# Both feed-forward output projections of a two-block transformer, by column halves with seven-product pairs

## The chip, the cores and the metric

The kernel runs on one core of a Trainium2 chip. The metric is the device time of one execution in microseconds. TensorE (PE) does the matrix products, VectorE (DVE) and ScalarE (ACT) the element-wise work, GpSimd (POOL) issues the DMAs that add while they write, and SyncE (SP) issues most loads.

## What is computed

The reference is two transformer blocks at 256 tokens and width 2048, all in float32: mixers, cross-attention and a feed-forward network in each, with a scaled residual and a layer norm behind each. The parts that matter here are the output projections of the feed-forward networks (inner width 5632):

```python
# first block
h = x @ ffn_in
gate, up = split(h, 2)
gate = causal_conv3(gate) + conv_b
ff = (silu(gate) * up) @ ffn_out            # [256, 5632] @ [5632, 2048]
x = layer_norm(2 ** 0.25 * x + ff, g, b)
# second block
y = (silu(x @ w1) * (x @ w3)) @ w2          # [256, 5632] @ [5632, 2048]
x = layer_norm(2 ** 0.25 * x + y, g, b)
```

## The kernel before

**Units.** Every weight matrix is read in units of 512 rows by 512 columns (1 MiB). SP loads a unit into one of four slots of `wraw`; ACT writes its rounded high part into `whi` (`hi`, line 748); DVE subtracts and writes the low part into `wlo` (`lo`, line 2005); PE multiplies. A product in full precision takes three passes: high by high, high by low, low by high. A whole unit of the output projection is 4 row chunks by 2 token tiles (of 128 tokens) by 3 passes, 24 matmuls of 128x512 (line 1288, in `products`). Slot reuse ties the engines together: the high part of unit n waits until PE has finished unit n - 4 (`unit_done`), the load of unit n until the low part of n - 4 is written (`lo_done`). All engines run their instructions in order, and each engine's order is written out by hand.

**Input projections.** The hidden layer is made in eleven blocks of 512 features. From the second block on, seven products of half-size blocks stand for eight (`seven_products`, `part_products`, line 1409): some units hold weights that are sums of two weight blocks, made by POOL with an adding DMA (lines 1988 and 1990) or by DVE (`part_a <- part_a, wraw`), and some products take mixes of the activations (`mix_x`, `mix_h`, `mix_l`). Each block is written to `hidden_dram` by `send_hidden` (line 986).

**Output projection, before.** `ffn(...)` ends with eleven pieces of four units. Piece n is the hidden block n, read back into one of two `h_stage` tiles (`load_stage`, line 990, on ACT's queue), copied to the high part `f_h` (line 2546) and subtracted to the low part `f_l2` by `split_piece` on DVE. A piece is multiplied with four units, one for each 512 output columns (`cb` 0 to 3), into eight banks of PSUM, two a column block. All eight banks fill over the 44 units, so the results of all columns come at the end. DVE then adds them to the residual (`joined`, line 2181, in the first block; line 3003 in the second), takes the statistics (lines 2177, 3004) and normalises (lines 2203 and 2208; 3011 and 3012). In the first block four joins stand one behind each of the last four units, and between them three low parts of the next stage. In the second block the last four units are multiplied for the first token tile first and then for the second, so that DVE can finish the first tile meanwhile.

`dve.link` is an instruction with a wait for its own completion. `to_act` (DVE) is this:

```python
def to_act(ins):
    ins.then_inc(shifted, 1)
    lo_to(ahead[0])
    dve.wait_ge(mapped, w.at("mapped"))
```

Of the kernel before, what the change touches and what calls it, by code (L numbers as in the profile page):

```python
# [21 lines left out]
P = 128  # L22
T = 256
# [25 lines left out]
          ("mix_out", 16), ("xq", 4), ("xv", 4), ("xo", 4), ("ffn_in", 8 + 11 * (FB - 1)), ("ffn_out", 4 * FB),  # L49
          ("gates2", 1), ("mlstm", 16), ("mlstm1", 16), ("dilated", 24), ("out2", 16), ("x2", 48), ("xo2", 16),  # L50
          ("ffn2_in", 8 + 11 * (FB - 1)), ("ffn2_out", 4 * FB)]
# [14 lines left out]
def part(layer, i, j):  # L66

    return BASE[IN[layer]] + 8 + 11 * (i - 1) + j

# [137 lines left out]
def two_blocks(nc, a, tables, out):  # L207
    tab_at, _ = shape_tables()
    ctx = ExitStack()
    with ctx:  # L210
# [5 lines left out]
        def sem(name):  # L216
# [29 lines left out]
                   "x3": (X0, Y1), "x4": (Y1 + 12 * KB, Y1 + 20 * KB), "x5": (Y1 + 12 * KB, Y1 + 20 * KB),  # L246
                   "y": (X0, Y1)}
# [89 lines left out]
        up_t = place("up_t", Y1 + 20 * KB, [P, NT, UNIT])  # L337
        h_stage = [place(f"h_stage{n}", X0 + (8 + 4 * n) * KB, [P, CB, T]) for n in range(2)]
# [103 lines left out]
        first_tap = sem("first_tap")  # L442
        taps_made = sem("taps_made")
# [115 lines left out]
        def _(sp):  # L559
# [84 lines left out]
            def ffn(layer, gate, up, up_c, down):  # L644
# [27 lines left out]
                for cb in range(NB):  # L672
                    if cb == 0:
                        sp.wait_ge(fourth_sum_made, nth(layer, FB - 1))
                    else:
                        sp.wait_ge(lo_done, part(layer, FB - 1, (0, 6, 9, 11)[cb]))
                    load(rows(down, 0, cb * UNIT))
                with sp.Fori(1, FB) as i, w.loop(i, 1, FB - 1, {"unit": 4}):
                    for cb in range(NB):
                        load(down[bass.ds(i * UNIT, UNIT), cb * UNIT:(cb + 1) * UNIT].rearrange("(k p) n -> p k n", p=P))  # L680
# [55 lines left out]
        def _(act):  # L736
# [251 lines left out]
            def load_stage(layer, n):  # L988
                act.wait_ge(hidden_out, 16 * (FB * layer + n + 1))
                act.dma_start(h_stage[n % 2][:, :, :], hidden_dram.ap()[n]).then_inc(stage_in[n % 2], 16)  # L990
# [39 lines left out]
            def ffn(layer, following):  # L1030
# [22 lines left out]
                for i in range(1, FB):  # L1053
                    last = i == FB - 1

                    def next_high(j):
                        hi(1) if last else hi_part(layer, i + 1, j)
# [26 lines left out]
                    next_high(1)  # L1084
                    next_high(2)
# [7 lines left out]
                for n in range(2, FB):  # L1093
                    act.wait_ge(hidden_ready, FB * layer + n - 1)
                    load_stage(layer, n)
                    hi(1)
                    if n == 2 and not layer:
                        copy_up_and_tap(FB - 1, (4, 5), (6, 7))
                    hi(1)
                    if n == 2:  # L1100
                        if layer:
                            copy_hidden(FB - 1, (6, 7))
                        else:
                            map_taps(FB - 1)
                    elif n == 3 and not layer:
                        send_product(FB - 1)
                    hi(2)
                    if n == 4:
                        gains_for(following)
                        if following == "x3":  # L1110
                            small(b_hot[:, :], tab("hot")[0:REL, :])
                            small(b_rel[:, :], a["rel_bias_2"])
                hi(4)
# [141 lines left out]
        def _(pe):  # L1255
# [465 lines left out]
            def ffn(layer, first_of):  # L1721
# [9 lines left out]
                def piece(fresh, last, parity):  # L1731
                    pe.wait_ge(hidden_ready, w.at("hidden"))
                    for cb in range(NB):
                        if fresh:
                            if cb == 0:
                                pe.wait_ge(gates_kept, nth(layer, FB - 1))
                                pe.wait_ge(gates_read, nth(layer, FB - 1))
                            elif cb == 1:
                                pe.wait_ge(ups_read, 2 * nth(layer, FB - 1))
                                if not layer:  # L1740
                                    turn_block(layer, FB - 1, (4, 5), (6, 7))
                            elif cb == 2:
                                if layer:
                                    turn_block(layer, FB - 1, (), (6, 7))
                                else:
                                    pe.wait_ge(turned_copied, 2 * (FB - 1))
                            elif layer:
                                pe.wait_ge(turned_copied, 2 * nth(layer, FB - 1))
                            else:
                                pe.wait_ge(taps_made, CB * FB)  # L1750
                        products(T_BLOCK, 1, f_h[parity], f_l2[parity], cb * 1024, fresh=fresh, last=last)

                piece(True, False, 0)
                with pe.Fori(0, FB // 2 - 1) as i, w.loop(i, 0, FB // 2 - 1, {"unit": 8, "hidden": 2}):
                    piece(False, False, 1)
                    piece(False, False, 0)
                piece(False, False, 1)
                if not layer:
                    piece(False, True, 0)
                    return  # L1760
# [1297 lines left out]
```

## Time and profile before

| | |
|---|---|
| median of 3 runs | 3223.89 us (3223.07 to 3224.68) |
| the profiled execution's own time | 3227.49 us |
| its span in the trace | 3225.5 us |
| granted TensorE clock | 0.997 of full speed |
| busy: PE, DVE, ACT, POOL | 99%, 70%, 45%, 2% of the span |
| mean DMA rate | 220 GB/s |

The span runs from the first to the last instruction that the profile shows. Matmul ends are modelled and overlap, so that the distance from one matmul's start to the next says what a stream costs, not the length of one.

### The profile page before, as it was taken

To read this page: it belongs to the slowest core of one execution; us is meant where nothing else is said; L and a number is where in the kernel's file an instruction comes from. 1 tells how busy PE (TensorE), PEld (TensorE's weight loads), DVE (VectorE), ACT (ScalarE), POOL (GpSimd) and SP (SyncE) were. 2 spreads that over 40 slices of the span, in tenths; PEclk is the share of its full clock that TensorE was granted. 3 is DMA by queue.
4 is the path that set the end of the run, shared out by engine and by line. 5 is a ranking of instruction groups with operands and counts; after the bars stand their busy time and mean duration, and the time that the engine had idled before them with its cause. 6 is when DMAs were issued, how large, how long until landed. Compare 5 with 4: busy or idle time off the path is not lost.

```text
span 3225.5 us, 37942 instructions
## 1 busy us (share of the span) xinstructions
PE 3184.1 (99%) x16157; PEld 2696.9 (84%) x16157; DVE 2244.0 (70%) x1857; ACT 1442.4 (45%) x1032; POOL 52.2 (2%) x44
## 2 busy tenths in 40 slices
PE   9999999999999999999999999999999999999998
PEld 8888888888888888888888888888888888888886
DVE  7565566667678888885565786775555888888456
ACT  4333555433335666653333443343333555555332
POOL 0000000000000000000000000000000000000000
PEclk9999999999999999999999999999999999999999
DMA  8644556678558888877646455655546698888763
GB/s 315 214 166 159 196 183 228 216 261 294 174 195 250 268 262 265 255 249 246 221 156 223 151 180 199 219 208 170 170 170 209 192 277 259 262 260 282 250 216 114
DMA packets 312494, 708.34 MB, mean 220 GB/s; under 512 B 12392, under 2 KB 18324, under 8 KB 301332
## 3 DMA queue, kind: packets, MB, share of 16 engines
q1 hardware_dynamic: 270000, 587.50, 52.5%
q0 software_dynamic: 21120, 41.95, 7.4%
q10 hardware_dynamic: 21220, 76.66, 6.3%
q8 instruction: 118, 1.93, 0.2%
q14 instruction: 36, 0.29, 0.0%
HBM read 675.65 MB, written 30.41 MB: 219 GB/s over the span
## 4 chain that ended last, share of the span: by engine, by line
PE 92%; DVE 5%; DMA 1%; ACT 1%; issue 0%; ACTq 0%; DVEq 0%
PE ps L1409 44%; PE ps L1288 43%; PE ps L1283 4%; PE ps L1413 2%; DVE wlo L2005 1%; DMA wraw<-in_xattn_v 0%; DMA part_a<-in_ffn_in 0%; DVE tok L2241 0%; DVE tok L2246 0%; ACT whi L748 0%; DVE wlo L2509 0%; DVE tok L3012 0%; DVE act_hl L2069 0%; DVE tok L3011 0%; DMA s_b<-in_sg_ln_b 0%
## 5 line engine op out<-in xcount | busy, mean ns | idle before, releaser
L2005 DVE TENSOR_TENSOR wlo<-wraw,whi 128x2048 fp32r<-128x2048 f32 (+1 forms) x389 | 879.8, 2275 | 465.5 <-ACT whi L748 462.0
L748 ACT ACTIVATE whi<-wraw 128x2048 fp32r<-128x2048 f32 (+1 forms) x389 | 735.5, 1901 | 921.6 <-PE ps L1288 609.6
L1288 PE MATMUL ps<-whi,act_hl 128*128 128x512 f32 x2128 | 661.7, 392 | 1.4 <-DVE wlo L2005 1.1
L1409 PE MATMUL ps<-whi,act_hl 128*128 128x512 f32 x1808 | 557.2, 389 | 1.8 <-DVE f_b L2069 1.8
L1288 PEld LDWEIGHTS ps<-whi,act_hl 128*128 128x128 f32 x2128 | 396.1, 188 | 84.3 <-issue 1.9
L1288 PE MATMUL ps<-wlo,act_hl 128*128 128x512 f32 x1064 | 414.4, 389 | 0.0
L1409 PEld LDWEIGHTS ps<-whi,act_hl 128*128 128x128 f32 x1808 | 338.9, 188 | 73.2 <-DVE f_b L2069 2.2
L1409 PE MATMUL ps<-wlo,act_hl 128*128 128x512 f32 x904 | 351.8, 389 | 0.0
L1409 PE MATMUL ps<-act_hl,whi 128*128 128x512 f32 (+2 forms) x1376 | 306.8, 360 | 0.6 <-DVE m_k L2116 0.6
L2509 DVE TENSOR_TENSOR wlo<-wraw,whi 128x2048 fp32r<-128x2048 f32 x120 | 274.5, 2288 | 33.6 <-ACT whi L983 32.3
L983 ACT ACTIVATE whi<-wraw 128x2048 fp32r<-128x2048 f32 x120 | 230.0, 1916 | 150.3 <-PE ps L1409 131.4
L1409 PEld LDWEIGHTS ps<-act_hl,whi 128*128 128x128 f32 (+1 forms) x1376 | 240.0, 191 | 36.0 <-DVE m_k L2116 0.7
L1288 PE MATMUL ps<-whi,f_h 128*128 128x512 f32 x672 | 261.7, 389 | 0.2 <-DVE gate_t L2069 0.2
L1288 PE MATMUL ps<-wlo,f_h 128*128 128x512 f32 x672 | 261.5, 389 | 0.0
L1288 PE MATMUL ps<-whi,f_l 128*128 128x512 f32 x672 | 261.4, 389 | 0.0
L1288 PEld LDWEIGHTS ps<-wlo,act_hl 128*128 128x128 f32 x1064 | 199.7, 188 | 42.0
L1288 PE MATMUL ps<-whi,alt_hl 128*128 128x512 f32 x736 | 227.6, 390 | 0.0
L2509 DVE TENSOR_TENSOR wlo<-part_a,whi 128x2048 fp32r<-128x2048 f32 x80 | 183.3, 2291 | 61.5 <-ACT whi L983 60.8
L983 ACT ACTIVATE whi<-part_a 128x2048 fp32r<-128x2048 f32 x80 | 153.1, 1914 | 114.4 <-PE ps L1409 69.6
L1409 PEld LDWEIGHTS ps<-wlo,act_hl 128*128 128x128 f32 x904 | 169.7, 188 | 35.2
L1409 PE MATMUL ps<-act_hl,wlo 128*128 128x256 f32 x1136 | 171.5, 283 | 0.0
L1409 PEld LDWEIGHTS ps<-act_hl,wlo 128*128 128x128 f32 x1136 | 157.3, 190 | 4.8
(361 smaller groups left out, 3831.1 us busy)
## 6 DMA issues: line engine op xcount, KB each, us to landing
wraw<-in_w_in SPq DMA_DIRECT2D x118, 1024.0 KB, 5.4
wraw<-in_w SPq DMA_DIRECT2D x112, 1024.0 KB, 5.3
wraw<-laid_narrow_units SPq DMA_DIRECT2D x68, 1024.0 KB, 4.9
wraw<-in_ffn_in SPq DMA_DIRECT2D x68, 1024.0 KB, 7.4
wraw<-in_ffn_out SPq DMA_DIRECT2D x44, 1024.0 KB, 5.1
wraw<-in_w_branch SPq DMA_DIRECT2D x16, 1024.0 KB, 5.1
wraw<-in_w_mix_out SPq DMA_DIRECT2D x16, 1024.0 KB, 7.1
wraw<-in_w_out SPq DMA_DIRECT2D x16, 1024.0 KB, 5.3
```

The source lines that it names most:

```text
L748: act.activation(whi[:, slot, k, c], wraw[:, slot, k, c], ACT.Copy).then_inc(hi_done, 1)
L983: act.activation(whi[:, (g - 1) % SLOTS], part_raw(layer, i, j), ACT.Copy).then_inc(hi_done, 1)
L1283: ins = pe.matmul(o, wk, x, start=first and n == 0, stop=stop and n == 2, skip_group_check=True)
L1288: ins = pe.matmul(o, x, wk, start=first and n == 0, stop=stop and n == 2, skip_group_check=True)
L1409: return pe.matmul(o, left, right, start=start, stop=stop, skip_group_check=True)
L1413: return pe.matmul(o, src, ident[0:k, 0:k], start=True, stop=True, is_transpose=True, skip_group_check=True)
L2005: dve.tensor_tensor(wlo[:, slot, k, c], wraw[:, slot, k, c], whi[:, slot, k, c].bitcast(F32), ALU.subtract).then_inc(lo_done, 1)
L2509: dve.tensor_tensor(wlo[:, slot], part_raw(layer, i, j), whi[:, slot].bitcast(F32), ALU.subtract).then_inc(lo_done, 1)
```

## The change

Each output projection is done in two column halves, x = 0 (columns 0 to 1023) and x = 1 (1024 to 2047), of 28 units each. In a half, seven of the eleven hidden blocks (0, 1, 4, 5, 6, 9, 10) are whole pieces with two units of 24 matmuls. The other four make two pairs, (2, 3) and (7, 8). A pair with its two column blocks is a product of 2 by 2 blocks (two token tiles, two hidden blocks, two column blocks), and is done in seven products of 12 matmuls instead of eight. Units 4, 6, 7, 9, 11, 13, 14 of a half belong to the first pair and 18, 20, 21, 22, 24, 25, 26 to the second. The four banks of the half gather the sums of products for the result; the other half's four banks are the spare ones and gather the products that enter several results. At the end of the half `combine` on DVE adds and subtracts the spare sums into `tok`, together with the residual; `join` adds the half's own banks.

The weights of a pair: SP loads two blocks into `sum_o` and `part_c`; POOL adds a block to each with an adding DMA; DVE adds a third and fourth to `sum_o` (`add_to_sum`). The high part of a piece moves from DVE to ACT (`piece_rounded`, `pair_rounded`), and the activation mixes of a pair are made on DVE (`pair_low`), rounded on ACT (`mixes_rounded`) and subtracted on DVE (`out_mixes_low`). The hidden blocks are read back once for each half, 22 a projection instead of 11.

The core of the diff:

```diff
-          ... ("ffn_out", 4 * FB),
+          ... ("ffn_out", 2 * 28),
+WHOLE_AT = ((1, 2), (3, 5), (8, 10), (12, 15), (16, 17), (19, 23), (27, 28))
+SEVEN_AT = ((4, 6, 7, 9, 11, 13, 14), (18, 20, 21, 22, 24, 25, 26))
+WHOLE_PIECES = (0, 1, 4, 5, 6, 9, 10)
+SEVEN_PIECES = ((2, 3), (7, 8))
# SP, for each half x
+    if x: sp.wait_ge(out_fourth_made, seven_nth(layer, 0, 1))
+    load_whole(0, 0); load_whole(0, 1); load_first(0); load_second(0); load_whole(1, 0)
+    ...
+    load_whole(3, 0)
+    sp.wait_ge(out_third_made, seven_nth(layer, x, 0))
+    load(rows(down, SEVEN_PIECES[0][1] * UNIT, c0))
+    load_second(1)
# ACT
 def load_stage(layer, n):
+    piece = n % FB
+    act.wait_ge(hidden_out, 16 * (FB * layer + piece + 1))
+    if n > 1:
+        x, used = divmod(n - 2, FB)
+        if used in WHOLE_PIECES:
+            act.wait_ge(hidden_ready, whole_nth(layer, x, WHOLE_PIECES.index(used)))
+        else:
+            g = used // 5
+            act.wait_ge(pair_ready, seven_nth(layer, x, g))
+            act.wait_ge(out_mixes_made, seven_nth(layer, x, g))
# ACT, for each half x
+    load_stage(layer, begun + 2); piece_rounded(layer, x, 1); hi(1)
+    load_stage(layer, begun + 3)
+    ...
+    pair_rounded(layer, x, 0); hi_sum(layer, x, 0, 2)
+    load_stage(layer, begun + 4); load_stage(layer, begun + 5); mixes_rounded(layer, x, 0)
+    hi_sum(layer, x, 0, 3); hi(1); piece_rounded(layer, x, 2)
+    ...
+    hi(1); hi_sum(layer, x, 1, 1); pair_rounded(layer, x, 1)
+    load_stage(layer, begun + 9); load_stage(layer, begun + 10); mixes_rounded(layer, x, 1)
+    hi(1); piece_rounded(layer, x, 5)
# PE, for each half x
+    piece(0, 0)
+    if x: pe.wait_ge(combined, 2 * layer + 1)
+    else: pe.wait_ge(ups_read, 2 * nth(layer, FB - 1)); turn_block(layer, FB - 1, (4, 5), (6, 7))
+    piece(0, 1); piece(1, 0)
+    if x: pe.wait_ge(columns_joined, 2 * layer + 1)
+    pe.wait_ge(pair_ready, seven_nth(layer, x, 0))
+    seventh(tokens_in_pair(0, 0), spare, 0)
+    piece(1, 1)
+    if x: pe.wait_ge(columns_joined, 2 * layer + 2)
+    pe.wait_ge(out_mixes_ready, seven_nth(layer, x, 0))
+    seventh(mix(0), spare + 3, 0); seventh(mix(2), spare + 1, 0)
+    ...
# DVE
+def pair_low(layer, x, g):
+    dve.wait_ge(pair_high, 2 * m)
+    (two tensor_tensor subtractions into pair_l, the second signals pair_ready)
+    (four linked tensor_tensor subtractions into out_x, the last signals out_mixes_made)
+def combine(layer, x):
+    (waits for unit 24; eight linked 128x512 operations)
# DVE, for each half x
+    piece_low(layer, x, 1); lo(1)
+    pair_low(layer, x, 0); lo_sum(layer, x, 0, 2); out_mixes_low(layer, x, 0)
+    ...
+    lo(3); lo_sum(layer, x, 1, 1); pair_low(layer, x, 1); out_mixes_low(layer, x, 1)
+    lo(1); piece_low(layer, x, 5)
+    ...
+    lo_sum(layer, x, 1, 5); lo(1); add_to_sum(layer, x, 1, 6, out_fourth_made); lo_sum(layer, x, 1, 7)
+    piece_low(layer, x, 6); lo(2); combine(layer, x)
+    if x == 0:
+        lo(1); piece_low(layer, 1, 0); lo(2)
+        for half in range(2):
+            join(layer, 0, half, columns_joined)
+            statistics(tok, half)
+            if half == 0: lo_sum(layer, 1, 0, 1)
# POOL, for each half and pair
+    pool.wait_ge(out_c_in, ...);  part_c += block  (out_second_in)
+    pool.wait_ge(lo_done, out_unit(layer, x, SEVEN_AT[g][0]));  sum_o[g] += block  (out_first_in)
# DVE, behind the first block's projection
-    for cb in range(NB):
-        joined(tok, cb, ...)
-        statistics(tok, cb)
-        if cb < NB - 1: lo_to(w.now("unit") + 1 + cb)
+    lo_to(BASE["gates2"] + 1)
+    for half in range(2):
+        join(0, 1, half, sums_read)
+        statistics(tok, 2 + half)
+        if half == 0: lo_to(BASE["gates2"] + 2)
     ahead[0] = BASE["gates2"] + 3
     norm("x3", tok, act_h, act_l, ...)
# DVE, behind the second block's projection
-        for cb in range(NB):
+        for cb in range(2, NB):
```

## Rows read from the trace of the kernel before

**Rows 1.** The page: span, busy time and instructions of two engines.

```profile
span 3225.5 us, 37942 instructions
PE 3184.1 (99%) x16157; PEld 2696.9 (84%) x16157; DVE 2244.0 (70%) x1857; ACT 1442.4 (45%) x1032; POOL 52.2 (2%) x44
```

**Rows 2.** The chain that ended last (start, length, what): both output projections and their ends.

```profile
1308.27 40.82 PE ps L1409 x180
...
1428.36 233.98 PE ps L1288 x1032
1662.34 0.02 issue
...
2984.17 206.76 PE ps L1288 x912
3190.94 10.89 PE ps L1409 x48
```

**Rows 3.** Windows: an input projection's blocks, then the output projection (second block).

```profile
core 0: us, PE busy (x) PEld busy (x) DVE busy (x) ACT busy (x) POOL busy (x), PEclk, DMA share, GB/s
2652.00:2902.00 250.00, 250.00 (x1129) 207.45 (x1128) 206.94 (x121) 144.98 (x102) 15.60 (x12) 1.00 0.89 265
2984.00:3190.00 206.00, 206.00 (x911) 170.56 (x910) 103.56 (x56) 73.19 (x40) 0.00 (x0) 1.00 0.63 216
```

**Rows 4.** DMA queues, 1093 to 1349 us (six blocks of the first input projection); issues, KB, us to landing.

```profile
q1 hardware_dynamic: 25357, 50.36, 55.9%
q0 software_dynamic: 6336, 12.58, 28.3%
q10 hardware_dynamic: 864, 3.15, 3.0%
...
part_c<-in_ffn_in POOLq DMA_DIRECT2D x6, 1024.0 KB, 13.8
```

**Rows 5.** Tile `h_stage`: its DMAs' time to landing over the whole run (22 DMAs).

```profile
DMA to landing us min/median/max: 5.0/5.3/10.9
```

**Rows 6.** Timeline of DVE: low parts, old split of a piece, add, join, statistics.

```profile
1386.94 2.29 DVE L2069 TENSOR_TENSOR part_a<-part_a,wraw 128x2048 f32<-128x2048 f32 x1
1413.54 0.69 DVE L2546 CAST f_h<-h_stage 128x1024 fp32r<-128x1024 f32 x1
1414.27 1.22 DVE L2069 TENSOR_TENSOR f_l<-h_stage,f_h 128x1024 fp32r<-128x1024 f32 x1
1415.53 4.49 DVE L2005 TENSOR_TENSOR wlo<-wraw,whi 128x2048 fp32r<-128x2048 f32 x2
...
1646.05 1.22 DVE L2181 SCALAR_TENSOR_TENSOR tok<-tok,ps 128x1024 f32<-128x1024 f32 x1 [1.14 <-PE ps L1288]
1647.30 1.43 DVE L2177 BATCH_NORM_STATS2 bst<-tok 128x6 f32<-128x512 f32 x2
```

**Rows 7.** Timeline of DVE at the end of the first block's projection.

```profile
1659.64 2.29 DVE L2005 TENSOR_TENSOR wlo<-wraw,whi 128x2048 fp32r<-128x2048 f32 x1
1662.37 1.22 DVE L2181 SCALAR_TENSOR_TENSOR tok<-tok,ps 128x1024 f32<-128x1024 f32 x1 [0.43 <-PE ps L1288]
...
1665.67 0.17 DVE L2196 TENSOR_SCALAR rstd<-mv 128x2 f32<-128x2 f32 x1
1666.11 0.17 DVE L2197 RECIPROCAL rstd<-rstd 128x2 f32<-128x2 f32 x1 [0.27 <-ACT rstd L776]
```

**Rows 8.** Timeline of ACT: the high part of a unit, and an operation of a piece's size.

```profile
1389.27 1.93 ACT L983 ACTIVATE whi<-part_a 128x2048 fp32r<-128x2048 f32 x1 [2.88 <-DVE part_a L2069]
1402.80 1.07 ACT L1024 ACTIVATE h_block<-h_block 128x1024 f32<-128x1024 f32 x1 [3.19 <-DVE h_block L2558]
```

**Rows 9.** Timeline of DVE at the kernel's end.

```profile
3201.93 0.69 DVE L3003 SCALAR_TENSOR_TENSOR tok<-tok,ps 128x512 f32<-128x512 f32 x1 [1.30 <-PE ps L1409]
3202.65 0.69 DVE L3004 BATCH_NORM_STATS2 bst<-tok 128x6 f32<-128x512 f32 x1
3203.38 0.26 DVE L3005 BATCH_NORM_AGGREGATE mv<-bst 128x2 f32<-128x24 f32 x1
...
3210.10 0.68 DVE L3003 SCALAR_TENSOR_TENSOR tok<-tok,ps 128x512 f32<-128x512 f32 x1
...
3215.90 0.26 DVE L3005 BATCH_NORM_AGGREGATE mv<-bst 128x2 f32<-128x24 f32 x1
```

More of the change, by code:

```diff
@@ L1092, in ffn @@
                     next_high(4)
-                for n in range(2, FB):
-                    act.wait_ge(hidden_ready, FB * layer + n - 1)
-                    load_stage(layer, n)
+                for x in range(2):
+                    begun, spare = FB * x, 4 * (1 - x)
+                    load_stage(layer, begun + 2)
+                    piece_rounded(layer, x, 1)
                     hi(1)
-                    if n == 2 and not layer:
+                    load_stage(layer, begun + 3)
+                    if x + layer == 0:
@@ L1098, in ffn @@
                         copy_up_and_tap(FB - 1, (4, 5), (6, 7))
-                    hi(1)
[L1100 to L1105, printed above, removed]
+                    elif x == 0:
+                        copy_hidden(FB - 1, (6, 7))
+                    pair_rounded(layer, x, 0)
+                    hi_sum(layer, x, 0, 2)
@@ L1729, in ffn @@
                     seven_products(layer, i)
[L1731 to L1751, printed above, removed]
@@ L1758, in ffn @@
                 if not layer:
-                    piece(False, True, 0)
                     return
-                pe.wait_ge(hidden_ready, w.at("hidden"))
+                pe.wait_ge(hidden_ready, whole_nth(1, 1, 6))
                 for h in range(NT):
-                    for cb in range(NB):
-                        unit = w.now("unit") - NB + cb + 1 if h else w.at("unit")
+                    for half in range(2):
+                        unit = w.now("unit") - 1 + half if h else w.at("unit")
@@ L2550, in taps, with join @@
+            def join(layer, x, half, signal):
+                cb = 2 * x + half
+                dve.wait_ge(unit_done, out_unit(layer, x, WHOLE_AT[6][half]))
+                tt(tok[:, cb], tok[:, cb], two(ps[:, cb * 1024:cb * 1024 + 1024]), ALU.add).then_inc(signal, 1)
             def taps(n, gate, dst):
@@ L2647, in ffn @@
                     next_low(4)
[L2648 to L2649 removed]
+                for x in range(2):
+                    piece_low(layer, x, 1)
                     lo(1)
[L2651 removed]
+                    if x + layer == 0:
                         taps(FB - 1, turned_gate((6, 7)), h_block)
[L2653 to L2657 removed]
@@ L2661, in _ @@
+                w.at("unit", out_unit(layer, 1, 28) - w.now("unit"))
             for q in range(NB):
```

407 lines of the change are left out of this document (356 added, 51 removed).

## Prediction

> **What bounds the kernel now.** I read the page first: PE is busy 99% of the span, DVE 70% [rows 1]. Then the chain that ended last, at the two places that the change touches. From 1428.36 the chain is PE alone for 1032 matmuls in 233.98 us, and from 2984.17 for 912 in 206.76: 0.2267 us a matmul, with no gap [rows 2]. (One matmul lasts 0.39 us in the lists, but they overlap; the pitch is the cost.) So a whole unit costs 24 x 0.2267 = 5.44 us of PE, a unit of a seven-product pair 2.72 us. The windows say how much room the others have: beside the output projection DVE is busy 103.56 of 206 us and DMA 0.63 of its time; beside the input projection, where seven products stand for eight already, DVE 206.94 of 250 and DMA 0.89, and PE still has no gap [rows 3]. The clock is full in both, so no clock effect is in the sum.
>
> **What is removed.** Before, 44 x 24 = 1056 matmuls a projection; after, per half 14 x 24 + 14 x 12 = 504, so 1008. 48 fewer, 10.9 us each, 21.8 us for both projections.
>
> **Is there still room?** Per half PE has 504 x 0.2267 = 114.3 us. DVE's prices: a low part follows the next by 2.20 us (two in 4.49), an add of the same size 2.2, a piece's low part 1.2, join 1.25, statistics 1.46 [rows 6]; a linked 128x512 operation 0.72 (3201.93 to 3202.65, [rows 9]). Per half: 28 low parts 61.6, four adds 8.8, two mix low parts 4.4, seven piece low parts 8.4, two pairs of 2 x 1.2 + 4 x 0.72 = 10.6, combine 8 x 0.72 = 5.8; 99.6 us, and 5.4 more for joins and statistics at x = 0. That is 92% of PE's time. DMA: in six input blocks 48 loads of SP take 55.9% of 256 us, 3.0 us each; 12 adding ones 28.3%, 6.0 us each; six of 0.5 MiB 3.0%, 1.3 us each [rows 4]. A half has 22, 4 and 11 of these: 65.6 + 24.1 + 14.1 = 103.8 of 114.3 us, 91%. The sums fit, barely, so what counts is the order.
>
> **Walk through a half.** Time 0 is the start of unit 1; ends at full pace: unit 8 at 35.4, 14 at 57.2, 18 at 76.2, 21 at 87.1, 24 at 98.0, 25 at 100.7, 26 at 103.4, 27 at 108.9, 28 at 114.3. A high part (1.9 us, [rows 8]) of n can start at the end of n - 4. I go by these and by the orders of the front.
>
> *Entry, x = 0.* The old split of piece 0 loses its 0.7 us copy on DVE; the stage of block 3 is requested when piece 1's low part is ready, about 6 us in, and its pair is wanted by unit 4 at 16.3 (later in the first block, by the 1.75 us of turns). With a landing of 5 to 8 us it fits. Its taps (3.2 us) fit too. Cost 0.
>
> *Second pair.* Low part 18 ends at 57.2 + 1.9 + 2.2 = 61.3; pair low parts and mixes to 66.5. Only then is block 9's stage requested. Landing L, rounding 1.05, low part 1.2: ready at 68.9 + L against unit 19 at 76.2. Free up to L = 7.3, else L - 7.3 in each of the four halves.
>
> *From half 0 to half 1.* From unit 21's end DVE has no rest: high 25 to 89.0, low 25 to 91.3, add to 93.5, high 26 to 95.4, low 26 to 97.6, piece 6 to 98.8, low parts 27 and 28 to 103.2, combine to 109.0, low 29 and piece 0 to 112.4, low 30 and 31 to 116.8, join and statistics to 119.5, low 32 to 121.8, join and statistics to 124.5, low part of piece 1 to 125.7. PE wants that for unit 31 at 125.2: 0.5 us late. Worse is what waits behind it: ACT requests the stage of block 3 only after this signal (its buffer held piece 1), in order on its queue. It lands at 125.8 + L; rounding 1.05, low part 1.25: the pair is ready at 128.2 + L, while PE wants it for unit 32 at 130.6. The whole stall is L - 2.4, once a projection. The trace bounds L: 5.0 at least, 5.3 in the middle, 10.9 at most [rows 5], so 2.6 to 8.5. An adding DMA and a unit's load are under way just then, so not the middle of the quiet stage: I take 6.3, a stall of 3.9. Behind it the mixes are ready at +7.8 and wanted at +8.2.
>
> Here a page of the Trainium skill differs: DMA: Bandwidth & Descriptors (Anatomy of one DMA) fits a DMA at about 2.0 us plus bytes by 436 GB/s, for 0.5 MiB an estimate of 3.2 us. By that estimate the stall would be 0.8 and the two projections 6.2 us shorter than in my sum. No landing of this tile came under 5.0 [rows 5], so I don't take it.
>
> *Exit, first block.* Before, DVE was ready when the last unit ended: join at 1662.37, chain until 1662.34 PE [rows 2, 7]. Now two joins with low parts between them: combine ends at 109.0, next stage's low part 111.2, join and statistics 113.9, low part 116.1, and only then the last join: 1.7 late. And one low part fewer stands in that loop, so `to_act` in the norm, with `ahead` = third unit, finds one to do: 2.2 us between the variance and its reciprocal, which were 0.44 apart [rows 7]: 1.8 more. Together 3.5 us on the chain, since the flips wait for the normalised tiles.
>
> *Exit, second block.* Before, PE ended the first tile at 3201.83 and DVE set the end from there: a join at once, the norm, at 3210.10 the second tile's four joins and statistics, at 3215.90 the rest [rows 2, 9]. PE's last 48 matmuls (to 3212.7) were hidden; now the last 24. In this half's time: combine ends 109.0 as PE ends the first tile (108.9); two joins with statistics 2.9, norm 6.7, two joins 2.9, rest 9.6: 131.1, 16.8 behind PE's last matmul; before 3225.5 - 3212.7 = 12.8. So 4.0 of the 10.9 are not seen.
>
> **The sum.** First block -10.9 + 3.9 + 3.5 = -3.5. Second -10.9 + 3.9 + 4.0 = -3.0. For small margins (mixes +0.4 us, block 9's stage, high 25 behind a load of 9 us) 1.0 us in all; bounds 0 and 3. Total -5.5 us: the profiled execution's 3227.5 becomes 3222.0, and the median, which lay 3.6 below it, 3218.4.
>
> **Rivals.**
>
> *The stalls vanish (better).* If L is short or DVE gets there earlier, only the exits remain: 21.8 - 4.0 - 3.5 = 14.3 us, 3209.6. For it: PE has no gap beside the seven-product input stage at DMA 0.89 [rows 3]. Against: there no stage is requested in the shadow of a signal two microseconds before its use. Chance 0.22, with everything between 3206 and 3215.
>
> *Stages land late (the other side).* The stage DMAs share the 16 engines with 91% of load. With landing L everywhere the cost is 2(L - 2.4) + 4(L - 7.3), the second term only above 7.3. It eats the 14.3 us at L = 8.0; slower than before by over 0.2% (6.4 us, about what a measurement of this kernel can tell from no change) it gets from L = 9.1. At the 10.9 of [rows 5]: 17.0 + 14.4 - 14.3 = 17 us longer, 3241. For: adding DMAs took 13.8 us at 28% of the engines' time [rows 4]. Against: median 5.3. Chance 0.21.
>
> The Trainium skill, DMA: Bandwidth & Descriptors (SWDGE vs HWDGE vs iDMA), says that an engine goes round-robin between its queues, which speaks for a stage that lands after a third of the others' backlog, not behind all of it. No row here separates that from a single line.
>
> *Only part of the load gives way.* Weights of the pairs are late: POOL adds `part_c` first, 13.8 us to landing, then `sum_o`. For unit 34 (unit 6 of x = 1) the load is issued near 98 and landed near 107, added by 122, wanted at 132: ten to spare. At `sum_o` low 32 ends 121.8, added by 132, wanted near 138. This case needs DMA some 6 us later than in the input stage, and would add 2 to 5 us: 3221 to 3224. It and my forecast make the middle, 0.57.
>
> *It does not do what it says*: then PE would not have 96 matmuls fewer than 16157, the transposes aside. I see nothing for it; under 0.01.
>
> **How the numbers follow.** Forecast 3218.4; its own range is 3215 to 3222 (L from 5.0 to 7.5, margins 0 to 3). Range for 8 in 10: from 3208, just below the first rival's 3209.6, up to 3231, L near 9.5. The 0.2% bounds are 3217.4 and 3230.3. The first rival's 0.22 and the short side of the middle, 0.20, are faster: 0.42. Same: 0.37 of the middle and 0.01. Of the late rival's 0.21 nearly all is slower; 0.01 is left for same: 0.20 and 0.38.
>
> **What would show it.** 96 matmuls fewer. In the chain, between the halves of each projection, PE waits for a DVE write of `pair_l` (a stall of 3 to 5 us at unit 32) and before it under 1 us for `f_l2`; elsewhere in the projections PE without a gap. DMA share near 0.9 and DVE over 0.85 in both. At the first block's exit one `wlo` between lines of the variance and its reciprocal, and the last join 1.7 us behind PE. At the end 22.2 us from the first tile's last matmul to the end of the span, against 23.7. Wrong would make it: landings of `h_stage` over 8 us, PE waits at units 19 or 20 of a half, or a wait for `part_c` or `sum_o`.

## The result, and the profile after

The changed kernel takes 3261.61 us in the median of 4 runs (3258.14 to 3264.58), before 3223.48 us (3222.85 to 3224.68): the ratio is 1.0118, with a 95% interval of 1.0105 to 1.0130. It is slower by 38 us. I had forecast 3218.4, in a range up to 3231. Medians and ratios, here and below, leave out three single executions in a far slower state (4538 to 7028 us). The page of the changed kernel, with what answers to [rows 1]:

```profile
span 3255.7 us, 37693 instructions
...
PE 3175.7 (98%) x16061; PEld 2685.3 (82%) x16061; DVE 2401.2 (74%) x1967; ACT 1544.6 (47%) x1116; POOL 72.7 (2%) x60
```

The work is what the change says: 16061 matmuls, 96 fewer. But [rows 2] had PE alone in the chain for 1032 and for 912 matmuls, and now PE waits. PE's timeline gives each wait in brackets, with what ended it; these are the first matmuls behind the large waits in the two projections:

```profile
1434.40 0.47 PE L1617 MATMUL ps<-whi,pair_h 128*128 128x512 f32 x1 [1.94 <-issue]
...
1501.77 0.79 PE L1496 MATMUL ps<-whi,f_h 128*128 128x512 f32 x1 [5.92 <-DVE f_l L2329]
...
1556.15 0.79 PE L1496 MATMUL ps<-whi,f_h 128*128 128x512 f32 x1 [3.69 <-DVE f_l L2329]
...
1567.79 0.76 PE L1617 MATMUL ps<-whi,pair_h 128*128 128x512 f32 x1 [4.35 <-issue]
...
1632.54 0.50 PE L1496 MATMUL ps<-whi,f_h 128*128 128x512 f32 x1 [2.16 <-DVE f_l L2329]
...
1682.25 1.97 PE L1621 MATMUL ps<-core,tok 128*128 128x128 f32 x8 [5.74 <-DVE tok L2468]
...
3068.78 0.79 PE L1496 MATMUL ps<-whi,f_h 128*128 128x512 f32 x1 [4.00 <-DVE f_l L2329]
...
3124.08 0.50 PE L1496 MATMUL ps<-whi,f_h 128*128 128x512 f32 x1 [3.15 <-DVE f_l L2329]
...
3135.75 0.77 PE L1617 MATMUL ps<-whi,pair_h 128*128 128x512 f32 x1 [5.90 <-issue]
```

In order of time these are unit 4 (first pair), units 19, 31 and 32 (pieces 5 and 1, first pair of half 1), unit 19 of half 1, and the flips at the first block's exit; in the second block units 19, 31 and 32 again. Unit 19 of half 1 waits there too, 1.8 us. The places are the same in both blocks, so this is order, not chance. The windows around two of them, and the one of the second block's projection that answers to the last of [rows 3]:

```profile
core 0: us, PE busy (x) PEld busy (x) DVE busy (x) ACT busy (x) POOL busy (x), PEclk, DMA share, GB/s
1490.00:1510.00 20.00, 14.07 (x56) 11.20 (x55) 15.13 (x10) 11.61 (x8) 0.00 (x0) 0.83 0.76 207
1540.00:1570.00 30.00, 21.96 (x84) 17.37 (x84) 19.84 (x18) 10.39 (x7) 2.57 (x2) 0.88 0.82 218
...
3000.00:3206.00 206.00, 191.18 (x818) 156.30 (x817) 166.20 (x104) 111.07 (x71) 7.70 (x6) 0.97 0.83 257
```

Two things are to be seen. DVE is busy 166.20 of 206 us and DMA 0.83: both have room left on average, as I had reckoned, and PE waits all the same. And the granted clock is lower where PE has waited: 0.83 and 0.88 over these two windows, where it was 1.00 before in the same ones.

Where the waits come from stands in the chain that ended last, here through units 17 to 32 of the first block:

```profile
1465.58 2.30 DVE part_a L2329
1467.90 12.30 DMA wraw<-in_ffn_out
...
1482.17 2.29 DVE wlo L2265
1484.47 2.20 DVE wlo L2840
...
1491.83 7.49 DMA h_stage<-hidden_dram
...
1501.77 7.18 PE ps L1496 x24
...
1528.69 14.38 DMA wraw<-in_ffn_out
...
1556.15 7.29 PE ps L1496 x24
1563.44 4.35 issue
1567.79 5.46 PE ps L1617 x12
```

The first cause: SyncE may load unit 17 only when DVE has made the first pair's fourth sum (the end of `part_a`, 1467.90). The load lands 12.30 us later, so low part 17, low part 18, the pair's low parts and the mixes are late, and only behind these is the stage of block 9 requested (1491.83), which lands 7.49 later. What that load shares the engines with is seen on GpSimd's queue: the adding DMA to `part_c`, issued 3.65 us ahead of it,

```profile
1464.25 1.28 POOL L2248 DMA_DIRECT2D part_c<-in_ffn_out  x1 [41.03 <-DMA part_c<-in_ffn_out]
```

and it is so in all four halves: adding DMAs at 1593.93, 3030.82 and 3161.96, unit 17's load 4.2 to 5.1 us behind each, landing after 11.4, 12.3 and 12.2 us. The second: unit 31's load is issued at 1528.69 and lands after 14.38 us, DVE stands idle, and the joins, low part 32 and piece 1 are all behind it. A unit of 24 matmuls then takes 7.18 or 7.29 us and not 5.44, one of 12 takes 5.46 and not 2.72. That is the lower clock: its matmuls start 0.42 us apart and not 0.2267.

```profile
1502.79 0.63 PE L1496 MATMUL ps<-wlo,f_h 128*128 128x512 f32 x1
1503.21 0.63 PE L1496 MATMUL ps<-whi,f_h 128*128 128x512 f32 x1
```

SyncE's queue shows what stands beside that second load:

```profile
1525.77 0.51 SPq L730 DMA_DIRECT2D part_a<-in_ffn_out  x1
1526.32 0.51 SPq L739 DMA_DIRECT2D part_c<-in_ffn_out  x1
1528.69 0.37 SPq L611 DMA_DIRECT2D wraw<-in_ffn_out  x1
```

Three loads of 1 MiB in three microseconds, behind two more (units 29 and 30, issued 1521.08 and 1525.36). No adding DMA is under way here; the next one is issued at 1540.73. The landings from 1400 to 1660 us, before:

```profile
wraw<-in_ffn_out SPq DMA_DIRECT2D x44, 1024.0 KB, 5.1
...
h_stage<-hidden_dram ACTq DMA_DIRECT2D x9, 512.0 KB, 5.3
```

and after:

```profile
wraw<-in_ffn_out SPq DMA_DIRECT2D x34, 1024.0 KB, 7.0
h_stage<-hidden_dram ACTq DMA_DIRECT2D x20, 512.0 KB, 6.8
...
part_c<-in_ffn_out POOLq DMA_DIRECT2D x4, 1024.0 KB, 13.3
```

The tile `h_stage` over the whole run of the changed kernel, which answers to [rows 5]:

```profile
DMA to landing us min/median/max: 3.5/6.7/9.5
```

For the sums I use two stretches that every kernel has. Stretch A runs from the chain's x180 piece of the eighth input block to the first matmul on `act_hl` behind the first exit: before 1350.84 to 1673.10, 322.26 us; after 1343.78 to 1686.79, 343.01. Stretch B runs from the x180 piece that starts at 2903.47 before (2918.65 after) to the end of the span: 322.03 and 337.05. So A is 20.8 us longer, B 15.0, and what lies between 1.5: 37.3 us, near the medians' 38.1. The two profiled executions are only 30 us apart, since the changed one was 7.1 us quicker up to the start of A, where nothing is changed.

### The profile page after: what moved, and what is told of

The parts are those of the page before. It is cut to its first block, busy times and chain, and to the rows that moved or that the text cites. A ratio compares the mean times of both kernels' runs of the same rounds, so it can differ in the third digit from the quotient of the medians.

```text
span 3255.7 us, 37693 instructions
## 1 busy us (share of the span) xinstructions
PE 3175.7 (98%) x16061; PEld 2685.3 (82%) x16061; DVE 2401.2 (74%) x1967; ACT 1544.6 (47%) x1116; POOL 72.7 (2%) x60
## 4 chain that ended last, share of the span: by engine, by line
PE 79%; DVE 12%; DMA 5%; ACT 2%; issue 1%; ACTq 0%; SPq 0%; DVEq 0%
PE ps L1617 43%; PE ps L1496 31%; PE ps L1491 4%; DVE wlo L2265 4%; PE ps L1621 2%; DMA wraw<-in_ffn_out 2%; DVE wlo L2840 1%; DMA h_stage<-hidden_dram 1%; DMA wraw<-in_w 1%; ACT whi L845 1%; DVE out_x_mix L2329 1%; DVE part_a L2329 0%; DMA part_a<-in_w 0%; DVE f_l L2329 0%; DVE pair_l L2329 0%
## 5 line engine op out<-in xcount | busy, mean ns | idle before, releaser
L2265 DVE TENSOR_TENSOR wlo<-wraw,whi 128x2048 fp32r<-128x2048 f32 (+1 forms) x373 | 842.4, 2273 | 282.6 <-ACT whi L845 279.0
L845 ACT ACTIVATE whi<-wraw 128x2048 fp32r<-128x2048 f32 (+1 forms) x373 | 703.9, 1900 | 694.4 <-PE ps L1496 330.5
L1496 PE MATMUL ps<-whi,f_h 128*128 128x512 f32 x432 | 172.0, 398 | 21.0 <-DVE f_l L2329 21.0
L1496 PE MATMUL ps<-whi,f_l 128*128 128x512 f32 x432 | 170.4, 395 | 0.0
L1496 PE MATMUL ps<-wlo,f_h 128*128 128x512 f32 x432 | 170.1, 394 | 0.0
```

The lines of the kernel that those rows point to most:

```text
L845: act.activation(whi[:, slot, k, c], wraw[:, slot, k, c], ACT.Copy).then_inc(hi_done, 1)
L1496: ins = pe.matmul(o, x, wk, start=first and n == 0, stop=stop and n == 2, skip_group_check=True)
L2265: dve.tensor_tensor(wlo[:, slot, k, c], wraw[:, slot, k, c], whi[:, slot, k, c].bitcast(F32), ALU.subtract).then_inc(lo_done, 1)
```

## The experiments

Times are medians; "before" is measured beside them on the same chip, and its median differs by up to 1 us between the chips (3222.6 to 3223.6), so small differences are to be taken from the ratios. The ledger, with stretches A and B as differences to before's 322.26 and 322.03:

| kernel | us | ratio to before (95%) | A | B |
|---|---|---|---|---|
| changed | 3261.6 | 1.0118 (1.0105 to 1.0130) | +20.8 | +15.0 |
| small adding DMAs | 3229.2 | 1.0019 (1.0009 to 1.0029) | +4.7 | +1.2 |
| small additions on DVE | 3241.1 | 1.0063 (1.0046 to 1.0080) | +9.9 | +4.6 |
| first pair of half 1 early | 3256.4 | 1.0107 (1.0090 to 1.0124) | +19.3 | +13.0 |
| third stage tile | 3243.9 | 1.0067 (1.0050 to 1.0084) | +10.8 | +4.7 |
| three together | 3235.0 | 1.0052 (1.0033 to 1.0071) | +8.3 | +3.1 |
| and a later `part_c` load | 3223.5 | 1.0000 (0.9990 to 1.0009) | +2.0 | -2.9 |
| and a late combine, exit in order | 3224.3 | 1.0003 (0.9993 to 1.0013) | -0.2 | -2.4 |
| column halves alone | 3227.5 | 1.0010 (1.0000 to 1.0020) | +1.9 | +2.5 |
| mended (no late combine) | 3221.1 | 0.9995 (0.9986 to 1.0004) | -0.3 | -1.7 |
| later `part_c` load alone | 3244.1 | 1.0063 (1.0050 to 1.0077) | +13.7 | +9.6 |
| mended, small adding DMAs | 3214.1 | 0.9971 (0.9960 to 0.9982) | -5.5 | -5.8 |

### The suspected load taken away: small adding DMAs

The 8 adding DMAs of each projection move one row chunk of four, so that part of the weight sums is left out. Order, waits and instructions stay.

```diff
-pool.dma_start(part_c[:, :, :], rows(down, q * UNIT, c1), accum_op=ALU.add).then_inc(out_second_in, 16)
+pool.dma_start(part_c[:, 0:1, :], rows(down, q * UNIT, c1)[:, 0:1, :], accum_op=ALU.add).then_inc(out_second_in, 16)
```

(and the same for `sum_o`)

> The adding DMAs of the output projections move one row chunk of four (the other three quarters of those weight sums are left out). Theory A, landings: the projections are late because unit loads issued in bursts land after 12 to 14 us under 0.8 to 1.0 of DMA load; with a fifth of that load gone the burst landings fall to about 9 us, unit 17's and unit 31's loads come 3 to 5 us earlier in each half, and the time falls by 10 to 20 us, to 3242 to 3252. Rival B, the DVE order: DVE is the queue that is late and the DMAs only look it; then the time falls by under 5 us, to 3257 or more. Rival C, the stage read behind the signal: about 4 us, from 7.5 us landings becoming 6.

Measured 3229.2, 32 us less: more than any of the three theories asked for. The landings between 1400 and 1660 us:

```profile
wraw<-in_ffn_out SPq DMA_DIRECT2D x35, 1024.0 KB, 5.5
h_stage<-hidden_dram ACTq DMA_DIRECT2D x20, 512.0 KB, 5.0
```

They are almost those of before. But the two loads that the theory named part ways. Unit 17's now lands after 7.4 us and not 12.3, with SyncE's loads ahead of it as they were, and the waits at unit 19 are gone:

```profile
wraw<-in_ffn_out SPq DMA_DIRECT2D x1, 1024.0 KB, 7.4
```

Unit 31's load lands as late as before, where 9 us had been expected,

```profile
1522.58 14.19 DMA wraw<-in_ffn_out
```

and at units 31 and 32 PE still waits 3.5 and 2.0 us (3.0 and 2.0 in the second block). So unit 17's load is late for the adding DMA beside it, and unit 31's for the burst of plain loads in which it is issued. The edit makes the adding DMAs themselves land sooner too (6.9 us for `part_c`); the changed kernel's chain through both projections waits for none of them.

### DVE relieved: small additions

The four additions of a pair of weights in each half work on 128x128 and not 128x2048, and the combine leaves out its additions to `tok`; these parts of the output are left out.

```diff
-tt(sum_o[g][:, :, :], sum_o[g][:, :, :], wraw[:, (n - 1) % SLOTS], ALU.add).then_inc(signal, 1)
+tt(sum_o[g][:, 0:1, 0:P], sum_o[g][:, 0:1, 0:P], wraw[:, (n - 1) % SLOTS, 0:1, 0:P], ALU.add).then_inc(signal, 1)
...
-scaled(0, 0, first_t, ALU.add)
-scaled(0, 1, w_t, ALU.subtract)
```

> DVE's four adds of a half shrink to 128x128, and combine keeps its first two operations and one of 128x128: 8.8 + 4 us of DVE work less in each half (most of two weight sums in seven and most of the combination are left out). Rival B, the DVE order: the adds release the loads of units 17 and 29, and combine stands before low part 29; so the chain shortens by 4 us at unit 19 of each half and 8 us between the halves, 20 to 30 us in all with the clock that comes back: 3232 to 3242. Theory A, landings alone: loads are issued 2 to 4 us earlier but land as late in the burst: under 8 us, 3254 or more.

Measured 3241.1, 20 us less, as rival B said. Unit 19 waits 2.0 and 1.0 us (5.9 and 4.0), unit 31 1.0 and 1.0 (3.7 and 3.2). At unit 32, where the mended DVE should have helped most, nothing is won (4.35 in the changed kernel; in the second block 6.15 for 5.90):

```profile
1562.85 0.77 PE L1617 MATMUL ps<-whi,pair_h 128*128 128x512 f32 x1 [6.36 <-issue]
```

When piece 1 is ready earlier PE gets to unit 32 earlier too, and waits there for the stage of block 3, which is requested behind that same piece. That wait is the landing, and DVE's speed doesn't touch it. At unit 19 the two reliefs overlap: of 13.9 us of waits in the four halves the small adding DMAs take nearly all and the small additions some 9.3, for they shorten the same chain, a load that frees a low part that frees a request. The totals say less: 32 + 20 us is more than the 38 by which the kernel is slower, but not more than its waits, lower clock and exits, some 58 us, of which 21.8 are hidden by the matmuls saved.

### The first pair of half 1 loaded early

SyncE issues this pair's two loads in half 0, behind unit 19's and unit 23's load, and no longer in the burst with units 29 to 31.

```diff
-load_first(0)
-load_second(0)
+if x == 0:
+    load_first(0)
+    load_second(0)
...
 load_whole(5, 0)
+if x == 0:
+    next_pair_first()
...
 load_whole(5, 1)
+if x == 0:
+    next_pair_second()
```

> Only SP's order: the two loads of the first pair of half 1 are issued in half 0 (behind unit 19's and unit 23's load) and not in the burst with units 29 to 31. Theory A: unit 31's load lands after 6 to 8 us and not 14.4, DVE's 2.8 us of waiting for it goes, the stall at unit 31 shrinks by 3 us in both projections: 5 to 8 us less, 3254 to 3257. Rivals B and C: within 2 us of the changed kernel, 3260 to 3263.

Measured 3256.4, 5 us less. At unit 31 the wait is 0.8 us in both blocks, from 3.7 and 3.2: the burst was the cause of that one, whose load now lands after 9.7 us. But in the first block unit 32 takes part of it back (in the second it stays at 5.87):

```profile
1569.64 0.76 PE L1630 MATMUL ps<-whi,pair_h 128*128 128x512 f32 x1 [6.23 <-issue]
```

### A third stage tile

Three stage reads (block 9 of half 0, blocks 3 and 9 of half 1) go to the place of `h_block`, which is free by then. Block 9 is requested with block 8, and block 3 of half 1 already with that half's first two blocks.

```diff
+EXTRA = (9, 14, 20)
...
-h_stage = [place(f"h_stage{n}", X0 + (8 + 4 * n) * KB, [P, CB, T]) for n in range(2)]
+h_stage = [place(f"h_stage{n}", X0 + (8 + 4 * n) * KB, [P, CB, T]) for n in range(2)] + [h_block]
...
-load_stage(layer, begun + 3)
+if x == 0:
+    load_stage(layer, begun + 3)
```

> A third stage tile (the place of h_block, free by then) takes blocks 9 of both halves and block 3 of half 1, so these three reads are requested early and no longer behind the low part that frees a tile. Rival C, the stage read behind the signal: unit 32's stall (4.35 and 5.9 us) and its slow-clock matmuls (2.7 and 2.2 us) go, unit 19 gains 0.9 us in each half: 14 to 18 us less, 3243 to 3248. Theory A: the read shares the same busy engines, but 10 us ahead, so the same. Rival B: as soon as the stage is in, DVE's own order keeps the pair late: under 6 us, 3256 or more.

Measured 3243.9, 18 us less. The wait at unit 32 is gone in both blocks, so the request behind the signal was its cause. Units 31 (4.6 and 4.1 us) and 19 (4.2 and 2.8) still wait, and the chain of this kernel names the load of unit 31, still in its burst (unit 17's still takes 12.2 us):

```profile
1532.35 15.32 DMA wraw<-in_ffn_out
```

### The two together, and DVE's order in the turn

As well, on DVE the low part of piece 1 of half 1 comes straight behind low part 32, ahead of the second join; the statistics of half 0 follow both.

```diff
 join(layer, 0, half, columns_joined)
 dve.wait_ge(columns_joined, 2 * layer + half + 1)
-statistics(tok, half)
 if half == 0:
     lo_sum(layer, 1, 0, 1)
+    piece_low(layer, 1, 1)
```

> Three edits together, output unchanged: the first pair's two loads of half 1 issued while half 0 runs (tried alone: 5 us less), a third stage tile for pieces 9 of half 0, 3 and 9 of half 1 (tried alone: 18 us less), and on VectorE the low part of piece 1 of half 1 put straight behind low part 32, ahead of the second join. Theory A (loads and stages are requested behind signals that come too late, and land late under the adding DMAs' load): the edits free different units (19, 31, 32), so their gains add: 3261 - 5 - 18 - 2 to 6 = 3232 to 3236. Every wait of PE at unit 32 gone, unit 31 under 1.5 us, unit 19 under 4. Theory B (VectorE alone is too full in the turn between the halves): the first two edits don't shorten VectorE's line, so only the order counts, 3236 to 3242, and unit 31 keeps over 2 us. Rival C (the three gains are one gain seen thrice, since every stall lets the queues catch up): 3241 to 3245, with new gaps at later units.

Measured 3235.0, as the first theory said, waits included. No wait at units 31 and 32 in the first block, and none in the second. What is left is unit 19, with the load of unit 17 in the chain ahead of it:

```profile
1465.94 13.39 DMA wraw<-in_ffn_out
```

and, in PE's timeline, unit 19 of half 1:

```profile
1617.82 0.79 PE L1531 MATMUL ps<-whi,f_h 128*128 128x512 f32 x1 [3.26 <-DVE f_l L2364]
```

### Unit 17's load ahead of `part_c`

One line of SyncE moves: the second pair's `part_c` load, which stood ahead of the loads of units 15 to 17, is issued behind unit 17's.

```diff
 load(rows(down, SEVEN_PIECES[0][1] * UNIT, c0))
-load_second(1)
 w.at("unit")
 load_whole(3, 1)
 load_whole(4, 0)
 sp.wait_ge(out_fourth_made, seven_nth(layer, x, 0))
 load_whole(4, 1)
+load_second(1)
```

> As the kernel with the three edits, and the second pair's part_c load on SyncE stands behind unit 17's load and not ahead of it. Theory A (unit 17's load is one of four in a burst and shares the engines): unit 17's load lands some 3 us sooner, unit 19's wait goes away, 3 to 6 us less than the kernel with the three edits: 3228 to 3232. Rival: the part_c load is then late for its adding DMA, units 20 to 24 wait, same time or up to 4 us longer.

Measured 3223.5: 11.4 us less, where 3 to 6 had been expected, and level with before. The load of unit 17 lands after 7.9 us and is no longer in the chain (an adding DMA of `sum_o` is, with 18.31 us from 1482.93, but PE waits only 1.0 us behind it), and within both projections no wait of PE is over 1.5 us. The edit moves more than one plain load: POOL's adding DMA to `part_c` waits for that load, and goes from 1462.30 to 1480.30, behind unit 17's landing. The first experiment tells the two apart: there the plain load stayed where it was, only the adding DMAs shrank, and unit 17 landed after 7.4 us. So what held it up was the adding DMA.

Alone on the changed kernel, the same line:

> The changed kernel with one line of SyncE moved: the second pair's part_c load behind unit 17's load. Theory A (the burst in front of unit 17's load is what makes unit 19 late): unit 19's gaps (5.9, 2.2, 4.0, 1.8 us) go, with the slow clock behind them: 3243 to 3250. Rival (the gain of 11 us came only because the three other edits had cleared the way; here stage 9 and unit 31 stay late): 3255 to 3262.

It measured 3244.1, 17.5 us less, as the first theory said and as much as the third stage tile by itself (17.7). Unit 17's load takes 6.4 us; in the second block no wait at unit 19 is over 0.6. The profiled execution, at 3247.3, is the slowest of its five, and that of the changed kernel the fastest of its four, so the traces show less of the gain than the medians. Unit 19 of this kernel, and unit 32, where nothing was changed:

```profile
1500.03 0.50 PE L1496 MATMUL ps<-whi,f_h 128*128 128x512 f32 x1 [0.38 <-DVE f_l L2329]
...
1564.33 0.77 PE L1617 MATMUL ps<-whi,pair_h 128*128 128x512 f32 x1 [6.46 <-issue]
```

The 5.92 us went to 0.38 for two reasons that have to be told apart: counted from the start of A, unit 19 starts at 154.97 us and not 157.99, 3.0 us sooner; and PE arrives there 2.5 us later, since in this execution it had waited 4.0 us at unit 4 and not 1.9. The rest of stretch A's 7.1 us is the unit 19 of half 1 (2.2 to 0.5 us) and the clock behind unit 19, which stays full.

### What is left in the turn and at the exit

On top of that: the combine of half 0 only frees the banks, and its additions to `tok` and the statistics go into half 1; at the first exit no low part stands between the joins or in the norm; the mixes of half 1's first pair have a place of their own.

```diff
+if x == 0:
+    return
...
-if half == 0:
-    lo_to(BASE["gates2"] + 2)
-ahead[0] = BASE["gates2"] + 3
-norm("x3", tok, act_h, act_l, (0, 0, 0, BASE["gates2"] + 4))
+ahead[0] = BASE["gates2"] + 1
+norm("x3", tok, act_h, act_l, (0, *(BASE["gates2"] + n for n in (2, 3, 4))))
```

> As the kernel before it, and in the turn between the halves the combine only frees the banks, while its additions to tok and the statistics of half 0 are put into half 1, where VectorE has time; at the first block's exit no low part stands between the joins or in the norm's rstd; the mixes of half 1's first pair have a place of their own. Theory A and B together: no wait of PE over 1 us is left within the projections, and the first exit loses 3 of its 6 us: 3212 to 3220. If the exit alone gives: 3222 to 3228. Rival (the engines' load of the adding DMAs, not the order, is the bound): gaps move to other units of half 1, sum of gaps unchanged, 3228 to 3234.

Measured 3224.3, a miss: nothing is won on the kernel ahead of it. PE waits at unit 19 of half 1 for 3.2 us (2.4 in the second block), and the chain shows the deferred statistics (`bst`) right there:

```profile
1610.93 0.70 DVE bst L2475
```

PE's timeline at that unit:

```profile
1615.14 0.50 PE L1534 MATMUL ps<-whi,f_h 128*128 128x512 f32 x1 [3.16 <-DVE f_l L2367]
```

Work taken from the crowded turn had been put where low part and piece of unit 19 are due. So the next kernel leaves the late combine out and keeps the exit and the place (the expectation calls the place unit 18; it is unit 19):

> As the kernel with the late part_c load (3223.5), and two more edits: at the first block's exit no low part stands between the joins and in the norm's rstd, and the mixes of half 1's first pair have a place of their own. The late combine of the ninth kernel is left out, since the two gaps of 3.2 and 2.4 us that PE had there at unit 18 of half 1 were not in the kernel before it. Theory (what is left of the loss is order): exit gap 5.8 us down to 3.6, gap at unit 32 gone, no 3 us gap in half 1: 3218 to 3221, faster than before by 0.1 to 0.2%. Rival (the gaps in half 1 came with the exit's order or the mixes' place, or the rest of the gain is lost to the clock): 3222 to 3225.

Measured 3221.1, 1.6 us under before; the interval of the ratio, 0.9986 to 1.0004, reaches over 1, so a gain isn't shown. The wait at unit 32, which should have gone, is 0.9 us in both blocks. The exit's timeline on DVE, where variance and reciprocal are again 0.44 apart as in [rows 7]:

```profile
1661.41 0.17 DVE L2494 TENSOR_SCALAR rstd<-mv 128x2 f32<-128x2 f32 x1
1661.85 0.17 DVE L2495 RECIPROCAL rstd<-rstd 128x2 f32<-128x2 f32 x1 [0.27 <-ACT rstd L906]
```

PE's waits there are 2.3 and 1.5 us for 5.2 and 0.7.

### The halves without the pairs

Each half takes its 22 units whole, with 22 stage reads and no adding DMA, weight sum or combine.

```diff
-("ffn_out", 2 * 28)
+("ffn_out", 2 * 22)
...
-WHOLE_PIECES = (0, 1, 4, 5, 6, 9, 10)
+WHOLE_PIECES = tuple(range(11))
```

> Column halves alone: 2 x 22 whole units for each projection, no pairs, no adding DMAs, no combine; 96 matmuls more than the changed kernel, 22 more stage reads than before. Theory A (what costs is the pairs' loads and adding DMAs): the halves cost only their two exits, worked out in the prediction at 3.5 and 4.0 us: 3223 + 5 to 9 = 3228 to 3232, PE without a gap inside the projections. Rival (the halves cost by themselves, through stages re-read behind signals and the crowded turn): gaps at the turn, 3236 or more. Then a pair would cost nothing.

Measured 3227.5, half a microsecond under what the first theory said: 4 us over before, with no wait of PE inside the projections, 3.1 and 0.7 us at the exit. The halves cost only their ends. The stage reads, twice as many, landed faster than any before:

```profile
DMA to landing us min/median/max: 3.1/3.3/8.0
```

### The load taken away once more, in the mended order

The mended kernel with the small adding DMAs of the first experiment (the same part of the sums is left out).

> The mended kernel with the projections' adding DMAs moving one row chunk of four (16 DMAs of 0.25 MiB and not 1 MiB; the sums are wrong by that part). Theory A in its strict form (it is the order, and after mending the adding DMAs' load costs nothing): within 2 us of the mended kernel. Rival (the engines' load stays a cost whatever the order; in the changed kernel the same cut gave 32 us): 5 or more below it, 3213 to 3216.

Measured 3214.1, 7.0 us under the mended kernel; the strict form of the theory (within 2 us) falls. The same cut was worth 32 us in the changed kernel's order. Order decides some 25 us of that, and 7 us remain a cost of the adding DMAs in the best order that I found.

## Why the prediction was wrong

The mechanism I named for the loss, stages and loads that land late and stall PE between the halves, is the rival to which I gave 0.21. Its places were right, but for unit 31, and its price was not: I had it at 17 us more at worst, since it priced the landings of stages alone, not those of unit loads, and no clock. By the steps, for both projections, from the changed kernel's trace:

| step | forecast | measured |
|---|---|---|
| matmuls | -21.8 | -21.8 (96 fewer) |
| entry | 0 | +3.2 (first block: 0.57, 1.93, 0.36, 0.32) |
| block 9's stage, unit 19 | 0 up to a landing of 7.3 | +13.9 (5.92, 2.16, 4.00, 1.77) |
| units 31 and 32 | +7.8 | +17.1 (3.69, 4.35, 3.15, 5.90) |
| exit, first block | +3.5 | +4.5 (wait for the first flip 5.74, before 1.23) |
| exit, second block | +4.0 | +5.0 |
| clock | 0 | +13.9 (what is left of A and B; 11.7 in five units) |
| between A and B | 0 | +1.5 |
| margins | +1.0 | in the others |
| sum | -5.5 | +37.3 |

**The pace of PE was right, and each exit but for 1 us.** The first exit's step of 1.8 us stands in the timeline of DVE as forecast, a low part between variance and reciprocal, 2.28 apart:

```profile
1676.98 0.17 DVE L2456 TENSOR_SCALAR rstd<-mv 128x2 f32<-128x2 f32 x1
1677.06 2.28 DVE L2265 TENSOR_TENSOR wlo<-wraw,whi 128x2048 fp32r<-128x2048 f32 x1
1679.26 0.16 DVE L2457 RECIPROCAL rstd<-rstd 128x2 f32<-128x2 f32 x1
```

The last join starts 2.9 us behind the end of PE's last unit (1673.68 and 1670.80), before 0.2, so it is 2.7 late where I had 1.7. At the end, which answers to [rows 9], DVE combines, joins a first time, and PE's last matmul follows:

```profile
3227.77 1.41 DVE L2329 TENSOR_TENSOR tile_t<-ps,tile_t 128x512 f32<-128x512 f32 x2
...
3233.57 0.69 DVE L2329 TENSOR_TENSOR tok<-tok,ps 128x512 f32<-128x512 f32 x1
...
3237.55 0.39 PE L1617 MATMUL ps<-wlo,f_h 128*128 128x512 f32 x1
```

From there to the end of the span are 18.2 us, against 13.2 before: 5.0 where I had 4.0. The 1 us is the same in both: the combine ends 1.2 us behind the matmuls ahead of the last 24, and I had it at 0.1.

**The step that failed at unit 19** was not the stage's landing: it took 7.5 us, hardly over the 7.3 that I had called free. It was the line "low part 18 ends at 57.2 + 1.9 + 2.2", which let ACT start high part 17 and 18 as soon as PE freed the slot. Unit 17's weights were not there. Low part 18 ended 9.2 us before PE wanted unit 19 (1486.7 and 1495.85), where my walk had 14.9. I had priced a unit's load at 3.0 us of the engines' time and never its landing. SyncE may issue this one only behind a sum of the pair (`out_fourth_made`, 1467.90), and it landed 12.3 us later, beside the adding DMA to `part_c`. With that adding DMA made small it lands after 7.4 us; with it moved behind, by way of the one `part_c` load, after 6.4, which gave 17.5 us.

**At units 31 and 32** I had DVE 0.5 us late and L = 6.3 for the stage. DVE was 3.7 late, for the load of unit 31 (14.4 us to landing); the stage took 8.0 (requested 1556.18, `pair_h` at 1564.24). With L = 8.0 my L - 2.4 is 5.6, less the 1.9 that the lower clock added to unit 31 ahead of it: 3.7, measured 4.35. The form of the sum, a request behind the signal that PE also waits for, held: a third tile removes the wait at 32, and the earlier loads that at 31.

**The clock** was missing from the sum, though a stall of 4 us was in it. I had written that the clock is full in both stretches; it was, because PE never paused there. Behind the five longest waits in the projections, 5.92, 3.69, 4.35, 4.00 and 5.90 us, the unit ran at the lower clock for a while and took 1.7, 1.9, 2.7, 3.2 and 2.2 us more than its price: 11.7 us. Behind the others, 1.77 to 3.15 us, a unit took at most 0.3 more. The remaining 2 us of the table's line are the flips at the exit (0.5) and some 0.2 us with which PE starts again behind each wait. The Trainium skill says on TensorE: Matmul & The Clock Gate (Part 1: The HAM clock gate): "the default state is throttled, and activity releases the throttle". The rows agree for the long waits (0.83 and 0.88 over the windows around them).

**The averages misled.** DMA at 91% and DVE at 92% of PE's time "fit, barely", I wrote, and went on with landings taken from a quiet stage. The engines' load was right, but at that load a unit's load lands after 11 to 13 us beside an adding DMA and after 14 to 15 in a burst of plain ones, and each is followed by 2 to 4 dependent steps. The adding DMAs lengthen the landings in the median too (7.0 us, 5.5 with small ones), the order decides whether anybody waits: 32 us against 7.

What stays open: how the 7 us that the adding DMAs still cost in the mended order divide between landings and the clock (in the profiled executions the wait at unit 4 falls from 3.5 to 1.6 us), and the wait at unit 4 of the first block, which was 1.0 to 4.0 us in kernels that don't differ there. Its chain begins with a load of 12.1 us at the entry (issued 1401.91), which holds up piece 1 and with it the request for block 3; I made no experiment on it. And the pairs themselves earn little even when mended: by the ratios (0.9995 and 1.0010) the mended kernel is some 5 us under the column halves alone, of 21.8 us of matmuls saved.

## What to carry to other kernels

When a queue hands out its loads behind signals, walk through the landings as through the engines' work: for each load the signal that allows it, what else is issued within a few microseconds, on other queues too (an adding DMA follows the load that it waits for), the landing that this makes (here 14 to 15 us in a burst and 11 to 13 beside an adding DMA, against 5.1 in the median before), and the time at which its user wants it. A request that waits for the same signal as its user is a stall of the whole landing; give it another buffer. And price a long stall of the engine that sets the pace with the slower clock behind it: here 11.7 us behind 23.9 us of waits, and next to nothing behind the shorter ones.

## What the runs showed of the hardware

A read of 0.5 MiB landed in 3.3 us in the median (3.1 at least) in the kernel of halves alone, where [rows 5] had nothing under 5.0. One of them, requested 5.9 us behind the last unit load and 2.8 ahead of the next, took 3.3; that the distance from the loads makes the difference wasn't tried by itself. In the changed kernel the same read took 6.7. I had refused an estimate of 3.2 us from the Trainium skill, DMA: Bandwidth & Descriptors (Anatomy of one DMA), because of [rows 5]. That page's fit is for DMAs that GpSimd issues, and this read is issued on ACT's queue; the 3.3 us of the halves agree with it all the same.

An adding DMA of 1 MiB (`part_c`) landed in 13.3 us in the median in the first block's projection, as in the input stage of [rows 4] (13.8), and one of 0.25 MiB in 6.9. A plain load of 1 MiB issued 3.7 to 5.1 us behind such a DMA of 1 MiB landed after 11.4 to 12.3 us in the changed kernel's four halves, behind one of 0.25 MiB after 7.4.

After PE had waited 5.15 us at an exit (the kernel with three edits and the later `part_c` load), the granted clock of the next 5 us was 0.50, the lower of its two levels:

```profile
1665.00:1670.00 5.00, 4.08 (x17) 3.38 (x18) 4.53 (x7) 1.14 (x2) 0.00 (x0) 0.50 0.36 136
```
